# Tail of the paged attention steps and its last join, up to the first unit of Wo: a new order on all queues

## What is computed

```python
q, k, v = diff_qkv(rmsnorm(h) , w_qkv)
# prompt: causal differential attention over its own 272 rows
# sample: 8 queries of each of 8 samples over 16 pages of 128 cached keys, and its own 8 new keys
p = softmax(scores - slope * dist);  a = p[:, :, 0] - lam * p[:, :, 1]
o = rmsnorm(a @ v, subln_g) * (1 - lam_init)
h = h + o.reshape(b, t, D_MODEL) @ w_o
h = h + swiglu(rmsnorm(h), ...)
```

## Time and profile before

| | us |
|---|---|
| median of 3 runs | 3141.52 (3141.25 to 3141.84) |
| the profiled execution's own time | 3140.64 |
| its span, first to last instruction | 3138.9 |
| PE busy | 3063.4 (98%) |
| DVE busy | 1494.1 (48%) |
| ACT busy | 1058.5 (34%) |
| mean granted clock of PE | 0.994 of full |

### The profile page before, as it was taken

The page is one execution under the profiler, slowest core; times in us unless marked ns, Lnnn a source line. Parts: engine busy times, 40 slices in busy tenths (PEclk is TensorE's granted clock), DMA queues, the critical chain, the costliest instruction groups (busy, mean ns, idle before and its releaser), DMA issues.

```text
span 3138.9 us, 60182 instructions
## 1 busy us (share of the span) xinstructions
PE 3063.4 (98%) x25406; PEld 2915.6 (93%) x25406; DVE 1494.1 (48%) x2153; ACT 1058.5 (34%) x1502; POOL 293.0 (9%) x233
## 2 busy tenths in 40 slices
PE   8999999999987999999999999999999999999998
PEld 7988888888865999999999999999999999999998
DVE  4434444444444554444444444456444444444445
ACT  3233433434333433222222222235332323323333
POOL 0022222222200110000000000014000000000002
PEclk9999999999999999999999999999999999999999
DMA  6499999999997554444444444443444444444442
GB/s 199 151 362 367 367 367 372 373 367 370 365 355 246 167 164 148 135 147 140 143 135 147 145 138 136 146 144 99 149 143 159 141 154 148 148 149 151 152 152 89
DMA packets 378808, 638.05 MB, mean 203 GB/s; under 512 B 15624, under 2 KB 261871, under 8 KB 377999
## 3 DMA queue, kind: packets, MB, share of 16 engines
q1 hardware_dynamic: 373984, 620.68, 57.3%
q0 software_dynamic: 3328, 11.24, 1.1%
q10 hardware_dynamic: 1230, 2.29, 0.2%
HBM read 625.37 MB, written 9.23 MB: 202 GB/s over the span
## 4 chain that ended last, share of the span: by engine, by line
PE 92%; DVE 4%; ACT 2%; issue 1%; DMA 1%; POOL 0%; SPq 0%; ACTq 0%; DVEq 0%; POOLq 0%
PE ps L1715 73%; PE ps L1826 7%; PE ps L1851 4%; PE ps L1876 3%; DVE halves L1152 1%; ACT halves L842 1%; PE ps L1976 1%; PE ps L1956 1%; PE ps L2126 0%; DMA io_tm<-in_x_sample_dram 0%; DVE keyT L1328 0%; PE ps L1865 0%; PE ps L1807 0%; DVE run L1344 0%; DVE pa_s L1428 0%
## 5 line engine op out<-in xcount | busy, mean ns | idle before, releaser
L1152 DVE TENSOR_TENSOR halves<-raw,halves 128x2048 fp32r<-128x2048 f32 x300 | 687.7, 2292 | 665.2 <-ACT halves L842 665.1
L842 ACT ACTIVATE halves<-raw 128x2048 fp32r<-128x2048 f32 x300 | 573.4, 1911 | 872.5 <-PE ps L1715 861.5
L1715 PE MATMUL ps<-xhi,halves 128*128 128x320 f32 (+1 forms) x3840 | 861.0, 311 | 4.8 <-DVE halves L1152 2.5
L1715 PE MATMUL ps<-yhi,halves 128*128 128x336 f32 x2816 | 657.2, 317 | 0.1
L1715 PEld LDWEIGHTS ps<-xhi,halves 128*128 128x128 f32 x3840 | 649.1, 188 | 6.2 <-issue 4.8
L1715 PE MATMUL ps<-xlo,halves 128*128 128x320 f32 (+1 forms) x1920 | 597.7, 311 | 0.0
L1715 PEld LDWEIGHTS ps<-yhi,halves 128*128 128x128 f32 x2816 | 483.1, 188 | 0.5 <-issue 0.4
L1715 PE MATMUL ps<-ylo,halves 128*128 128x336 f32 x1408 | 447.1, 318 | 0.0
L1715 PE MATMUL ps<-hA_hi,halves 128*128 128x336 f32 (+1 forms) x1408 | 375.5, 314 | 2.9 <-DVE hT L1606 2.9
L1715 PE MATMUL ps<-hB_hi,halves 128*128 128x336 f32 (+1 forms) x1408 | 372.8, 312 | 0.0
L1715 PEld LDWEIGHTS ps<-xlo,halves 128*128 128x128 f32 x1920 | 361.9, 188 | 0.1
(11 more groups left out here) (222 smaller groups left out, 3187.5 us busy)
## 6 DMA issues: line engine op xcount, KB each, us to landing
raw<-in_w_gate_up_dram SPq DMA_DIRECT2D x176, 1024.0 KB, 5.1
raw<-in_cache_k_dram SPq DMA_DIRECT2D x200, 512.0 KB, 6.8
raw<-in_cache_v_dram SPq DMA_DIRECT2D x194, 512.0 KB, 7.2
raw<-in_w_down_dram SPq DMA_DIRECT2D x88, 1024.0 KB, 5.0
kv_raw<-in_w_qkv_dram SPq DMA_DIRECT2D x64, 512.0 KB, 7.7
page<-in_cache_v_dram SPq DMA_DIRECT2D x62, 512.0 KB, 7.3
page<-in_cache_k_dram SPq DMA_DIRECT2D x56, 512.0 KB, 6.9
raw<-in_w_qkv_dram SPq DMA_DIRECT2D x16, 1024.0 KB, 5.2
```

The costliest lines, as they stand in the source:

```text
L842: act.activation(whi[t][:, :], raw[r][:, :], ACT.Copy).then_inc(hi_ready[t], 1)
L1152: dve.tensor_tensor(wlo[t][:, :], raw[r][:, :], whi[t][:, :].bitcast(F32), ALU.subtract)\
L1715: mm = pe.matmul(out, l, r, start=first and n == 0, stop=last and n == 2)
```

## The change

- The four joins' parts stand in another order. `factors` comes first in its step on DVE; `out_means` comes at the end of that step instead of in the next one; `out_normed` comes between the two key copies of the next step; `out_features` comes at the end of the next step instead of the one after it.
- Of the 16 input chunks four are turned in steps 124 to 127, one in each (`HX_AT`); the other twelve stand behind the loop between the parts of the last join, in three banks, 6, 7 and 4 (`HX_BANKS`).
- The loop ends with step 127. What steps 128 and 129 did is written out behind it.
- The loads of the input rows on POOL's queue stand in steps 113, 115, 117, 119 and 121 instead of 113, 114, 115, 116 and 118.
- Slots 0 and 1 take no page from page 125's keys on (`LESS_FROM`). SP loads Wo's unit 0 into them, ahead of the keys of page 127, and ACT and DVE split it straight behind step 127.

```diff
-HX0 = 122
-BACK_AT = (113, 114, 115, 116, 118)
+HX_AT = {124 + c: c for c in range(4)}
+HX_BANKS = (4, 4, 4, 4) + 4 * (6, 7, 4)
+BACK_AT = (113, 115, 117, 119, 121)
...
+        if t == PAGES - 2:
+            order.append(("o", 0))
...
+LESS_FROM = PAGE_LOAD["k", PAGES - 3, 0]
...
+        if n == LESS_FROM:
+            del last[0], last[1]
...
+                if kind == "o":
+                    for slot in range(2):
+                        page_used(max(n for n in range(len(IN_STEPS)) if PAGE_SLOT[n][0] == slot))
+                    load(cols256(wo, 0, 0), U_WO, dst=as8)
+                    continue
...
@@ POOL @@
-                if t - 1 in PAIR_AT:
-                    pool.wait_ge(o_ms, PAIR_AT[t - 1] + 1)
+                if t in PAIR_AT:
+                    pool.wait_ge(o_ms, PAIR_AT[t] + 1)
...
@@ ACT, behind the loop @@
+            act.wait_ge(k_stored, 48 * H)
+            act.wait_ge(v_stored, 48 * H)
+            act.wait_ge(pa_done, TILES)
             split_hi(U_WO)
+            probs_out(PAGES - GROUP - 1)
+            exps(PAGES // GROUP - 1)
+            for c in (4, 6):
+                back_features(c)
+            for v in range(PAGES - GROUP, PAGES):
+                probs_out(v)
+            for c in (8, 10):
+                back_features(c)
             out_squares(3)
+            for c in (12, 14):
+                back_features(c)
             out_features(3)
-            for c in (DC - 2, DC - 1):
-                act.wait_ge(*back_done(c))
-            act.wait_ge(pa_done, TILES)
+            b, k = hx_bank(DC - 1)
+            act.wait_ge(bank_full[b], bank_n("hx", b, k, True))
             act.wait_ge(o_out, 8)
...
@@ DVE, in the loop @@
+                if t in PAIR_AT:
+                    factors(PAIR_AT[t])
                 if t in KV_END:
                     kv_features(KV_END[t])
-                if t < PAGES:
-                    keys_out(t, 1)
+                keys_out(t, 1)
...
@@ DVE, behind the loop @@
+            split_lo(U_WO)
+            add_values(PAGES // GROUP - 2)
+            for c in (5, 7):
+                back_features(c)
+            add_sums(PAGES // GROUP - 1)
             factors(3)
+            back_features(9)
+            add_values(PAGES // GROUP - 1)
             out_means(3)
+            back_features(11)
             out_normed(3)
-            split_lo(U_WO)
+            for c in (13, 15):
+                back_features(c)
...
@@ PE @@
-                if p:
-                    pe.wait_ge(o_out, 2 * p)
...
+            turn_probs(PAGES - GROUP - 1)
+            for v in valued_in(PAGES):
+                values(v)
+            for c in range(4, 8):
+                turn_back(c)
+            for v in turned_in(STEPS - 1):
+                turn_probs(v)
+            for c in range(8, 10):
+                turn_back(c)
+            for v in valued_in(STEPS - 1):
+                values(v)
+            turn_back(10)
             join_halves(3)
+            for c in range(11, 15):
+                turn_back(c)
             turn_out(3)
+            turn_back(15)
```

More of the change, by code:

```diff
@@ L124, in page_order @@
                 order.append(("w", n))
+        if t == PAGES - 2:
+            order.append(("o", 0))
     return order
 PAGE_ORDER = page_order()
-IN_STEPS = [x + (half,) for x in PAGE_ORDER if x[0] != "w" for half in range(2)]
+IN_STEPS = [x + (half,) for x in PAGE_ORDER if x[0] in "kv" for half in range(2)]
 PAGE_LOAD = {what: n for n, what in enumerate(IN_STEPS)}
 MORE_FROM = PAGE_LOAD["k", KV_STEPS * H + 3, 0]
+LESS_FROM = PAGE_LOAD["k", PAGES - 3, 0]
 def page_slots():
@@ L516, in ready_n, with hx_bank @@
             return DC * (k // 2) + c + 1
+        def hx_bank(c):
+            return HX_BANKS[c], HX_BANKS[:c].count(HX_BANKS[c])
         def back_done(c):
-            return bank_free[4], bank_n("hx", 4, c) + 1
+            b, k = hx_bank(c)
+            return bank_free[b], bank_n("hx", b, k) + 1
         def kv_out(block):
@@ L662, in _ @@
                     n += 1
-            for j in range(RAW):
+            for j in range(1, RAW):
                 for half in range(2):
@@ L1009, in _ @@
             act.wait_ge(cleared, 5)
-            for t in range(STEPS):
-                if t < PAGES:
-                    keys_out(t, 0)
+            for t in range(PAGES):
+                keys_out(t, 0)
                 if t - 1 in NEW_AT:
@@ L1056, in _ @@
             act.wait_ge(x_ready, DC)
-            act.wait_ge(v_stored, 48 * H)
+            for c in range(DC - 3, DC):
+                act.wait_ge(*back_done(c))
             for u in range(17):
@@ L1483, in _ @@
                 if t - 1 in PAIR_AT:
-                    out_means(PAIR_AT[t - 1])
-                if t < PAGES:
-                    keys_out(t, 3)
+                    out_normed(PAIR_AT[t - 1])
+                keys_out(t, 3)
                 if t - 1 in NEW_AT:
@@ L1499, in _ @@
                     tile_join(tile_at(t, 1))
[L1500 to L1503, removed]
+                if t in HX_AT and HX_AT[t] % 2:
+                    back_features(HX_AT[t])
                 if t == min(NEW_AT) - 1:
@@ L1509, in _ @@
                     dve.wait_ge(padded, 8)
-                if t < PAGES:
-                    scores_out(t)
-                if t < PAGES and t % GROUP == GROUP - 1:
+                scores_out(t)
+                if t % GROUP == GROUP - 1:
                     maxima(t // GROUP)
@@ L1941, in turn_back @@
                     pe.wait_ge(nt_out, NB)
-                take("hx", b, c)
+                if c == len(HX_AT):
+                    pe.wait_ge(pa_done, TILES)
+                take("hx", b, k)
                 for t in range(3):
@@ L1986, in tile_back @@
                 mm.then_inc(pa_back, 1)
-            for t in range(STEPS):
+            for t in range(PAGES):
                 work = list(KV_AT.get(t, ()))
-                if t < PAGES:
-                    turn_keys(t, 0)
+                turn_keys(t, 0)
                 if t in KV_END:
@@ L2020, in _ @@
                     tile_scores(tile_at(t, 0))
-                if t < PAGES:
-                    scores(t)
-                for v in turned_in(t):
-                    if v >= PAGES - GROUP:
-                        turn_probs(v)
+                scores(t)
                 for v in valued_in(t):
```

47 lines of the change are left out of this document (19 added, 28 removed).

## The result

| | before | changed |
|---|---|---|
| median, us | 3141.68 (4 runs, 3141.25 to 3142.35) | 3119.13 (4 runs, 3116.04 to 3121.89) |
| the profiled execution's own time | 3140.64 | 3121.89 |
| its span | 3138.9 | 3120.1 |
| mean granted clock of PE | 0.994 | 0.997 |

The ratio of the runs is 0.9922, with a 95% interval of 0.9910 to 0.9933: 24.5 us less (21.0 to 28.3). The medians differ by 22.6 us. The forecast was 19.8 less, 3121.7, in a range of 3117.5 to 3128.5. The direction and the two places of the gain held; the forecast was 2.8 us (medians) to 4.7 us (ratio) short, and the ratio, put on the median of before, gives 3117.2, just under the range. One of the runs used further down, of the small matrices late and filled, took 4096.7 us at a mean clock of 0.687 and is left out of all figures.

What follows compares the result with a forecast made beforehand. TensorE, on 92% of the chain of waits, was taken as the bound. 13.0 + 7.6 - 0.8 = 19.8 us off 3140.64 gives 3120.8, plus 0.9 to the runs' median 3121.7; range 3117.5 to 3128.5.

Steps and rivals of the forecast that it cites:

- the steps: Steps 122 to 127: 34.6 us instead of 47.6, 13.0 gained, with ends of 15.2 and 9.9.
- The pushed key copies: First key copies in three steps, delayed by `factors` on DVE: 0.5 us each, 1.5 together.
- `out_means`: At the step's end on DVE, waiting for ACT's squares: costed at nothing, unless ACT is late by over a microsecond.
- the tail: From the end of step 127 to `xhi`: 12.9 us instead of 20.5, 7.6 gained, reaching Wo's unit 1.
- The values of the last group start at about E + 4.75: E is the end of step 127; the last four pages' values start 4.75 us later, after DVE's split, an addition and copies.
- the loads: Page, Wo unit 0 and input-row loads: costed at nothing because their lead hides them.
- the margin was thin at the last values: Page 127's values, the tightest load; rival that loads become the bound: two pages late, 3127.7 us, chance 0.18.
- the clock term: A fall of TensorE's clock may hit Wo's unit 1: a cost of 0 to 2.5 us, taken as 0.8.
- the case that was feared: Rival: clock falls in Wo's unit 1 and once in the steps, 1.7 + 2.5 us lost, 3125.9 us, chance 0.13.
- the better end: Forecast's fastest end, from the better end of steps 122 to 127 and no clock cost: 3118.5 us.

Runs made afterwards that it cites:

- small matrices late and filled: Changed kernel with `factors` back behind the second key copy, plus four unused matmuls ahead of layer 1's pooling products: median 3132.16 us (9 runs).
- kernel with late matrices: Changed kernel with `factors` back behind the second key copy of steps 122, 124 and 126: median 3142.19 us (10 runs).
- split late: Changed kernel, Wo's unit 0 still loaded early but split in its old place, ahead of ACT's last squares and behind DVE's last normed rows: median 3121.64 us.
- rows early: Changed kernel with the input-row loads back in steps 113, 114, 115, 116 and 118: median 3118.57 us (4 runs).

## Why the prediction was right or wrong

**Right: the steps.** "13.0 us gained" in steps 122 to 127: 13.7. The place of `factors` is the largest single cause, 5.1 us alone and 11.6 when it is undone, and undoing it brings the waits for `stage` back. The windows of before have a fall that the prediction did not list (0.73 from 960 to 965, behind the wait of 2.69); it is within the 47.6 us and so within the gain. The pushed key copies cost 0.40, 0.24 and 0.32 where 0.5 each was taken, within the two ends that the prediction gave them. `out_means` waits 0.34 us for ACT's squares in one step and nobody waits for it.

**Right in the number, in part by luck: the tail.** "7.6 us gained": 7.3. "The values of the last group start at about E + 4.75": E + 4.67. But the text put this down to a bank that waits for DVE's split. The exponentials were done at E + 1.6, and TensorE was busy without a break until the values began, with six chunk transpositions among it. The experiments say it twice: without the split in that place nothing starts earlier, with four chunks fewer ahead of them the values start 1.4 us earlier. That two different reckonings, DVE's row of work and TensorE's, end within 0.1 us of each other is luck. What the split's place really buys is 2.6 us, and the early load with it 7.8.

**Right: the loads.** Costed at nothing, and nothing it was. That the margin was thin at the last values was right too.

**Wrong: the clock term, "I take 0.8".** This is the term of the sum that failed. It was written as a cost, and only for unit 1. In the profile the fall came in unit 0, where the wait for unit 1 hides it (TensorE still waited 1.36 us there), so the term measured nothing; the case that was feared exists and costs 1.6 and 2.5 us, as two other kernels show. Besides, the changed kernel already entered step 122 0.80 us earlier, with the same order on TensorE up to there, since the fall of the clock behind the DVE wait of step 118 was shorter in that execution: that is chance, not gain. With these two, the 0.7 and -0.3 above and 0.15 between `xhi` and unit 1, 19.8 becomes 22.0, what the trace shows at the pooling products. A small slip stands in the range's account: the better end is 3118.7 by its own terms (2.2 and 0.8 under 3121.7), not 3118.5.

**Put at nothing without a reason: the clock outside the change.** The sum and the range took the rest of the kernel as fixed, with 0.9 us from the profiled execution to the median. Three runs of before within 0.6 us suggested that. Its 57 runs beside the experiments lay between 3136.6 and 3156.1. This is what took the ratio past the range: the last 2.5 us of the 24.5 are of this kind by elimination, since the trace shows 22.0 at the pooling products and the code is the same behind them. Which falls they are in these particular runs no profile shows. The interval of the ratio, 21.0 to 28.3 us, holds the 22.0 of the traces; it would not hold the forecast's 19.8. What stays open is whether the change moves the chance of a fall at the pooling products, 1100 us further on: the profiles are too few to say.

## What to carry to other kernels

When two engines hand work to each other at the end of a step, move the short preparations of the next hand-over to the head of the step, and ask for each wait removed which wait is next in line (here 0.8 us for the features). Count a wait of about 2 us on TensorE at its length and, in a bad execution, about as much again at the lower clock: with the misplaced matrices three waits of 6.3 us were followed by 6.6 us of clock, while two like them in the kernel before had no fall behind them. Before a difference of a few microseconds is believed or doubted, compare the distances between two fixed rows inside the changed stretch; they repeated within 0.7 us here, while the time of the whole kernel had several times that noise, part of it from one idle place a thousand microseconds away and part from waits ahead of the change.

## What the runs showed of the hardware

The granted clock can stay at its lower level under a TensorE that is busy without a break. In the pooling products it did for 7 and 17 us in two executions of the changed kernel, and in the kernel with late matrices, whose code is the same there, through all 28 us of them and 6 us beyond, each time entered behind the same 2.1 us of idleness. That idleness alone does not decide it: the profiles of before, of the split late and of the rows early had it too, and no fall. With four matmuls put into that place it stayed at the full level in all four profiles. While it was low, the six matmuls of one product took 1.62 us instead of 0.89, as the kernel with late matrices has it,

```profile
2132.72 1.62 PE L2162 MATMUL ps<-band,y_tm 128*128 128x144 f32 x6
```

In that kernel the clock was back 5 us into the next stage, whose matmuls are 336 columns wide; in the other profiles it came back within the stage. Why these products do not bring it back sooner was not tried. The Trainium skill, "TensorE: Matmul & The Clock Gate", section "What's actually happening", has the level follow how busy TensorE has lately been, by which such a stretch should have raised it early; the runs show otherwise. The section "Seeing it yourself" warns that recorded clock events can be unreliable and that the clock has been seen stuck at a low level; here the durations of the matmuls, 1.62 against 0.89, say the same as the recorded clock.
